# The first w_up weights move into tiles of y that come free earlier, and the first three products begin without the last pair of form tiles

## What is computed

```python
def layer(x, ...):
    h = rmsnorm(x, norm_mix_g)
    proj = einsum('btd,de->bte', h, w_in)
    ...                                   # RG-LRU and pooling branches
    y_mix = concatenate([y_lru, y_pool], axis=-1)
    x = x + einsum('bte,ed->btd', y_mix, w_out)        # w_out: 2048 x 2048
    h2 = rmsnorm(x, norm_mlp_g)
    f = relu(einsum('btd,df->btf', h2, w_up))          # w_up: 2048 x 8192
    x = x + einsum('btf,fd->btd', f * f, w_down)       # w_down: 8192 x 2048
```

## Time and profile before

| | |
|---|---|
| median of three runs | 1935.13 us (1933.71 to 1935.13) |
| the profiled execution | 1937.47 us, span 1935.4 us |
| TensorE matmul busy | 1900.8 us, 98% of the span |
| VectorE busy | 1125.7 us, 58% |
| ScalarE busy | 764.7 us, 40% |
| mean granted TensorE clock | 0.989 |
| w_up begins | 519.07 us into the span |

### The profile page before, as it was taken

How to read it: one execution, slowest core, us unless ns; L and a number is a source line. 1 busy time by engine, 2 the same in 40 slices (tenths; PEclk the granted TensorE clock), 3 DMA queues, 4 the chain that set the end, 5 groups by cost and what they waited for, 6 DMA issues and landing times.

```text
span 1935.4 us, 38521 instructions
## 1 busy us (share of the span) xinstructions
PE 1900.8 (98%) x15746; PEld 1897.7 (98%) x15746; DVE 1125.7 (58%) x1442; ACT 764.7 (40%) x1054; POOL 71.4 (4%) x135
## 2 busy tenths in 40 slices
PE   7999999999899999999999999999999999999997
PEld 7999999999899999999999999999999999999997
DVE  7777775454587777777777775443334444343334
ACT  6555533333344545445454453222222222222234
POOL 2000000200000000000000000000000000000000
PEclk9999999999899999999999999999999999999998
DMA  8233332444444444444444324333444443333333
GB/s 276 88 93 92 93 101 88 151 137 135 149 120 125 142 154 118 143 124 142 132 118 144 122 94 138 115 115 117 125 137 136 135 136 115 116 115 115 93 91 108
DMA packets 202936, 241.36 MB, mean 125 GB/s; under 512 B 10558, under 2 KB 186186, under 8 KB 202769
## 3 DMA queue, kind: packets, MB, share of 16 engines
q1 hardware_dynamic: 187904, 186.87, 32.7%
q0 software_dynamic: 14880, 52.32, 7.2%
HBM read 209.22 MB, written 30.45 MB: 124 GB/s over the span
## 4 chain that ended last, share of the span: by engine, by line
PE 95%; issue 2%; DVE 1%; DMA 1%; ACT 0%; POOL 0%; SPq 0%; ACTq 0%; DVEq 0%; POOLq 0%
PE ps L783 13%; PE ps L781 12%; PE ps L785 12%; PE ps L742 11%; PE ps L744 11%; PE ps L743 11%; PE ps L562 8%; PE ps L565 8%; PE ps L568 8%; PE ps L805 1%; PE ps L579 0%; PE ps L580 0%; PE ps L581 0%; DMA work_area<-in_state_pool_dram 0%; DVE h_low L1384 0%
## 5 line engine op out<-in xcount | busy, mean ns | idle before, releaser
L1712 DVE TENSOR_TENSOR d_low<-d_raw,d_high 128x512 fp32r<-128x512 f32 x256 | 176.7, 691 | 424.8 <-ACT d_high L1079 424.8
L781 PE MATMUL ps<-f_high,d_high 128*128 128x260 f32 x2048 | 411.8, 282 | 4.2 <-DVE resid L1722 4.2
L783 PE MATMUL ps<-f_low,d_high 128*128 128x260 f32 x2048 | 413.5, 283 | 0.0
L785 PE MATMUL ps<-f_high,d_low 128*128 128x260 f32 x2048 | 411.4, 282 | 0.0
L742 PE MATMUL ps<-forms,u_high 128*128 128x260 f32 x1344 | 380.9, 283 | 6.8 <-issue 6.8
L744 PE MATMUL ps<-forms,u_low 128*128 128x260 f32 x1344 | 380.6, 283 | 0.0
L743 PE MATMUL ps<-forms,u_high 128*128 128x260 f32 x1344 | 380.2, 283 | 0.0
L1079 ACT ACTIVATE d_high<-d_raw 128x512 fp32r<-128x512 f32 x256 | 161.5, 632 | 519.0 <-PE ps L785 519.0
L781 PEld LDWEIGHTS ps<-f_high,d_high 128*128 128x128 f32 x2048 | 315.9, 189 | 4.4 <-DVE resid L1722 4.4
L785 PEld LDWEIGHTS ps<-f_high,d_low 128*128 128x128 f32 x2048 | 316.7, 189 | 0.0
L783 PEld LDWEIGHTS ps<-f_low,d_high 128*128 128x128 f32 x2048 | 315.7, 189 | 0.0
(11 more groups left out here) (260 smaller groups left out, 2846.9 us busy)
## 6 DMA issues: line engine op xcount, KB each, us to landing
d_raw<-in_w_down_dram SPq DMA_DIRECT2D x256, 256.0 KB, 2.8
even_rows<-in_w_up_dram SPq DMA_DIRECT2D x32, 1024.0 KB, 6.6
odd_rows<-in_w_up_dram SPq DMA_DIRECT2D x32, 1024.0 KB, 5.7
raw<-in_w_in_dram SPq DMA_DIRECT2D x96, 256.0 KB, 2.8
f_spill<-f_out POOLq DMA_DIRECT2D x32, 520.0 KB, 7.1
scratch<-f_spill POOLq DMA_DIRECT2D x32, 520.0 KB, 4.6
raw<-in_w_out_dram SPq DMA_DIRECT2D x64, 256.0 KB, 2.8
x_spill<-x POOLq DMA_DIRECT2D x8, 520.0 KB, 3.0
```

The source lines that it names most:

```text
L781: pe.matmul(outs[a], wh, fh[:, kk, a * HALF:(a + 1) * HALF], start=opens, stop=False)
L783: pe.matmul(outs[a], wh, fl[:, kk, a * HALF:(a + 1) * HALF], start=False, stop=False)
L785: mm = pe.matmul(outs[a], wl, fh[:, kk, a * HALF:(a + 1) * HALF], start=False, stop=closes)
L1712: dve.tensor_tensor(d_low[:, s].rearrange("p k e -> p (k e)"), d_raw[:, s, :], d_high[:, s].rearrange("p k e -> p (k e)").bitcast(F32), AL ...
```

## The change

`y_high` and `y_low` are laid out anew for what comes after w_out, so that what is written first lies in the slots that come free first: even rows of w_up and weight slot 0 in the first four slots (free after unit 154), forms 6 behind them (free after 156, before 154), odd rows and weight slot 1 behind those (158), forms 7 last (160). The tiles of the later w_down stage move with them. In m=0 product r=3 comes ahead of r=2. Products at places 0, 1 and 2 run over pairs 0 to 6 first, and over pair 7 after all three; only then are their slots released. ScalarE makes weights_high(0) and (1), and VectorE weights_low(0) and (1), before the end of the last unit as far as their waits allow. `block_sums(0,5)` and `block_sums(0,6)` go from turns 3 and 4 to turns 5 and 6.

```diff
+def product_of(q):
+    m, place = divmod(q, PRODUCTS)
+    return m, (0, 1, 3, 2, 4, 5, 6)[place] if m == 0 else place
+def place_of(m, r):
+    return PRODUCTS * m + ((0, 1, 3, 2, 4, 5, 6).index(r) if m == 0 else r)
...
-FREE_Y = 2 * FORM_SET
+ROWS_BYTES = KP * 256 * 4
+FORMS6_AT = ROWS_BYTES
+ODD_AT = FORMS6_AT + -(-FORM_SET // 32) * 32
+FORMS7_AT = ODD_AT + ROWS_BYTES
...
+        even_rows = [at_byte(f"even_rows{b}", at, [P, KP, 256]) for b, at in enumerate((Y_HIGH_AT, W_AT))]
+        odd_rows = [at_byte(f"odd_rows{b}", at, [P, KP, 256])
+                    for b, at in enumerate((Y_HIGH_AT + ODD_AT, W_AT + ROWS_BYTES))]
-        slot_at = (Y_LOW_AT + FREE_Y, Y_LOW_AT + FREE_Y + 2 * KP * P * 4, W_AT + 2 * KP * 256 * 4)
+        slot_at = (Y_LOW_AT, Y_LOW_AT + ODD_AT, W_AT + 2 * ROWS_BYTES)
...   SyncE, rows of w_up
-                        sp.wait_ge(unit_used, 158 if i == 0 else 160)
+                        sp.wait_ge(unit_used, 154 if i == 0 else 158)
...
-                        sp.wait_ge(u_lo, PRODUCTS * (m - 2) + (4 if i == 0 else 7))
+                        sp.wait_ge(u_lo, PRODUCTS * (m - 2) + (7 if i else 6 if m == 2 else 4))
...   TensorE
-                for k in range(KP):
-                    if m == 0 and r == 0:
+                for k in tiles:
+                    if q < SLOTS:
                         pe.wait_ge(s_hi, 2 * k + 2)
                         pe.wait_ge(s_lo, 2 * k + 2)
...
+            for q in range(SLOTS):
+                product(q, range(KP - 1))
+            for q in range(SLOTS):
+                product(q, (KP - 1,))
+            for q in range(SLOTS, PRODUCTS * UP_PAIRS):
+                if q == PRODUCTS:
                     pe.wait_ge(mean_ready, 2)
-                for r in range(PRODUCTS):
-                    product(m, r)
-                    if m == 0 and r == 2:
+                product(q, range(KP))
+                if q == SLOTS:
...                       the L757 matmuls
...   ScalarE
                 if o == 6:
-                    act.wait_ge(unit_used, 154)
+                    act.wait_ge(unit_used, 156)
...
+                    if n == OUT_PAIRS - 1 and j == 6:
+                        weights_high(0)
...
+                    act.wait_ge(unit_used, (154, 158, 160)[q])
...
+            weights_high(1)
             x2_blocks(OUT_PAIRS - 1)
-            weights_high(0)
+            weights_high(2)
             forms_high(OUT_PAIRS - 1)
-            weights_high(1)
             x2_squares(OUT_PAIRS - 1)
-            for turn in range(2, PRODUCTS * UP_PAIRS):
+            copy_p1(0)
+            for turn in range(SLOTS, PRODUCTS * UP_PAIRS):
                 weights_high(turn)
                 up_copies(turn)
...   VectorE
+                    if n == OUT_PAIRS - 1 and j == 7:
+                        block_sums(0, 1)
+                        weights_low(0)
...
+            weights_low(1)
             x2_add(OUT_PAIRS - 1)
+            block_sums(0, 3)
             x2_sums(OUT_PAIRS - 1)
-            block_sums(0, 1)
-            weights_low(0)
+            weights_low(2)
             forms_low(OUT_PAIRS - 1)
-            block_sums(0, 3)
-            weights_low(1)
             squares_add(OUT_PAIRS - 1)
-            for turn in range(2, PRODUCTS * UP_PAIRS):
+            for turn in range(SLOTS, PRODUCTS * UP_PAIRS):
...
-                if r == 3:
+                if place == (3 if m else 5):
                     block_sums(m, 5)
-                if r == 4:
+                if place == (4 if m else 6):
                     block_sums(m, 6)
                 weights_low(turn)
-                if m >= 1 or r == 6:
+                if m >= 1 or place == 6:
                     up_sums(turn)
                 if turn == 5:
                     mlp_norm()
```

More of the change, by code:

```diff
@@ L198, in build @@
         sets = [at_byte(f"forms{o}", o * 2 * FORM_SET, [P, 2, FORMS, HALF], F32R) for o in range(6)]
[L199 to L208, removed]
+        late = [[at_byte(f"forms{o}_{part}", at + place, [P, FORMS, HALF], F32R)
+                 for part, at in (("high", Y_HIGH_AT), ("low", Y_LOW_AT))] for o, place in ((6, FORMS6_AT), (7, FORMS7_AT))]
+        s_high = [v[:, 0] for v in sets] + [v[0][:] for v in late]
+        s_low = [v[:, 1] for v in sets] + [v[1][:] for v in late]
+        even_rows = [at_byte(f"even_rows{b}", at, [P, KP, 256]) for b, at in enumerate((Y_HIGH_AT, W_AT))]
+        odd_rows = [at_byte(f"odd_rows{b}", at, [P, KP, 256])
+                    for b, at in enumerate((Y_HIGH_AT + ODD_AT, W_AT + ROWS_BYTES))]
         t_sum = at_byte("t_sum", AUX_AT, [P, KP, P])
-        slot_at = (Y_LOW_AT + FREE_Y, Y_LOW_AT + FREE_Y + 2 * KP * P * 4, W_AT + 2 * KP * 256 * 4)
+        slot_at = (Y_LOW_AT, Y_LOW_AT + ODD_AT, W_AT + 2 * ROWS_BYTES)
         u_high = [at_byte(f"u_high{b}", at, [P, KP, P], F32R) for b, at in enumerate(slot_at)]
@@ L215, in build @@
         f_out = [at_byte(f"f_out{b}", STAGE_AT + b * PAIR_BYTES, [P, 4, HALF]) for b in range(2)]
-        d_raw = at_byte("d_raw", Y_HIGH_AT + FREE_Y, [P, D_RING, UNIT])
-        d_high = at_byte("d_high", Y_HIGH_AT + FREE_Y + D_RING * UNIT * 4, [P, D_RING, 2, 256], F32R)
-        d_low = at_byte("d_low", Y_HIGH_AT + FREE_Y + 2 * D_RING * UNIT * 4, [P, D_RING, 2, 256], F32R)
+        d_raw = at_byte("d_raw", Y_HIGH_AT, [P, D_RING, UNIT])
+        d_high = at_byte("d_high", Y_HIGH_AT + ODD_AT, [P, D_RING, 2, 256], F32R)
+        d_low = [at_byte(f"d_low{b}", at, [P, 2, 256], F32R)
+                 for b, at in enumerate((Y_HIGH_AT + D_RING * UNIT * 4, Y_HIGH_AT + ODD_AT + D_RING * UNIT * 4,
+                                         Y_HIGH_AT + FORMS7_AT + FORM_SET + 16))]
         window_at = [W_AT] + [b * 2 * PAIR_BYTES for b in range(WINDOW - 1)]
@@ L716, in _, with product @@
                         out_unit(2 * b + half, j, half)
-            def product(m, r):
-                q = PRODUCTS * m + r
+            def product(q, tiles):
+                m, r = product_of(q)
                 form, bank_at = PRODUCT_FORM[r], 4 * (m % 2) + PRODUCT_BANK[r]
@@ L744, in product @@
                     mm = pe.matmul(out, wl, xh, start=False, stop=(k == KP - 1), skip_group_check=True)
-                mm.then_inc(u_used, 1)
-            for m in range(UP_PAIRS):
-                if m == 1:
-                    pe.wait_ge(mean_ready, 2)
-                for r in range(PRODUCTS):
-                    product(m, r)
-                    if m == 0 and r == 2:
[L753 to L759, removed]
+                if tiles[-1] == KP - 1:
+                    mm.then_inc(u_used, 1)
+            for q in range(SLOTS):
[4 more added lines that the diff above has]
+                if q == PRODUCTS:
+                    pe.wait_ge(mean_ready, 2)
+                product(q, range(KP))
+                if q == SLOTS:
+                    pe.wait_ge(sq_summed, OUT_PAIRS)
+                    pe.wait_ge(pair_evac, 12)
+                    for a in range(2):
+                        for t in range(2):
+                            mm = pe.matmul(ps[:, 4 + a, 0:HALF], ones[:], scratch[:, 2 + t, a * HALF:(a + 1) * HALF],
+                                           start=(t == 0), stop=(t == 1))
+                    mm.then_inc(total_ready, 1)
             for u, (seg, kp) in enumerate(D_UNITS):
@@ L777, in _ @@
                     for t in range(2):
-                        wh, wl = (w[:, u % D_RING, kk, t * P:(t + 1) * P] for w in (d_high, d_low))
+                        wh, wl = (w[:, kk, t * P:(t + 1) * P] for w in (d_high[:, u % D_RING], d_low[u % D_RING]))
                         outs = [ps[:, 4 * down_buf(seg) + 2 * t + a, 0:HALF] for a in range(2)]
@@ L994, in forms_high, with weights_high @@
                 act.activation(s_high[o][:, 4:FORMS, :], sums[:], ACT.Copy).then_inc(s_hi, 1)
+            def weights_high(q):
+                m, r = product_of(q)
+                if q < SLOTS:
+                    act.wait_ge(unit_used, (154, 158, 160)[q])
+                else:
+                    act.wait_ge(u_used, q - SLOTS + 1)
+                if r == 0:
+                    act.wait_ge(rows_in[0][m % 2], 16 * (m // 2 + 1))
+                elif r in (2, 4):
+                    act.wait_ge(rows_in[1][m % 2], 16 * (m // 2 + 1))
+                if r in t_ready:
+                    act.wait_ge(t_ready[r], m + 1)
+                act.activation(u_high[q % SLOTS][:], up_block(m, r), ACT.Copy).then_inc(u_hi, 1)
             for n in range(OUT_PAIRS):
@@ L1032, in f_free, with copy_p1 @@
                     act.wait_ge(blocks_ready, 2 * (OUT_PAIRS - 1 + m))
-            def up_copies(q):
-                m, r = divmod(q, PRODUCTS)
-                if r == 3:
[L1038 to L1041, removed]
-                    else:
-                        act.wait_ge(u2_ready, m)
-                    act.activation(p1_copy, ps[:, 4 * (m % 2) + BANK_A, 0:HALF], ACT.Copy).then_inc(p1_copied, 1)
-                if r == 4:
```

(66 more changed lines are left out.)

8 lines of the change are left out of this document (3 added, 5 removed).

## The result

The changed kernel took 1941.22 us (median of 9 runs, 1939.39 to 1943.92) beside 1935.13 us for the kernel before in the same comparison: a ratio of 1.003, 95% interval 1.0022 to 1.0039, 4.3 to 7.5 us. The forecast was 1935.5 us, range 1931.8 to 1938.5. The profiled execution took 1943.92 us, span 1941.9.

The account below looks back on a forecast made before the run. TensorE's matmuls bound the kernel; only waits could be won. Seam before: 6.99 wait + 2.8 clock = 9.8 us; after: 0.81 + 2.16 + 4.41 + clock 2.8 = 10.2. Difference +0.4, forecast 1935.5 us, range 1931.8 to 1938.5.

Parts of the forecast that it names:

- Part 1: End of w_out: weights 0 and 1 made early at no cost, 0.6 us ahead of x2_add(7); products 0, 1 start at once.
- A: TensorE's wait before product 2, for weights_low(2) on VectorE: 0.81 us.
- B: TensorE's wait before product 3, whose weights cannot begin until a slot comes free behind pair 7: 2.16 us.
- C: TensorE's wait before product 6, because block_sums(0,6) stands behind mlp_norm on VectorE: 4.41 us.
- Part 4: TensorE's granted clock at the seam: falls to 1.2 GHz behind C, losing 2.8 us (bounds 0 and 2.8).
- B's clock: Loss by a slow clock behind the wait at product 3: put at 0.
- a wait of 2.1 us: TensorE's existing wait at the kernel's end, after which the clock was read as still 1.00 at 1912 to 1913.
- 0.50 already at 525: Sign of being wrong: granted clock at 0.50 by 525 us, where the forecast had 1.00 from 514 to about 537.
- Rival (c): Seam: B brings the clock down too, C does not shrink; 2.8 us more, 1938.3 us; chance 0.15.
- (a): Seam: the clock does not fall in C, or only for a part; 1932.7 us; chance 0.14.
- The new places of the w_down tiles: w_down: moving its tiles adds or removes no instruction, so 0 us either way.

Follow-up runs that it names:

- e7: The kernel of e2 with a fourth weight slot, used once, for product 3's weights; 1930.77 us, ratio 0.9977 to the kernel before.
- e2: The changed kernel with mlp_norm cut in three, its later operations moved behind turns 12 and 19; 1934.44 us, ratio 0.9994 to the kernel before.
- e1: The kernel before with only the tile layout of the changed kernel, every order of work as before; 1939.01 us beside 1935.51, ratio 1.0019.
- e5: The kernel of e2 with all that the change put into y_high and y_low 96 bytes further on; 1933.56 us, ratio 0.9988 to the kernel before.
- e6: The kernel of e2 with w_down's tiles dealt out otherwise in the same regions; 1934.78 us, ratio 0.9992 to the kernel before.
- e8: The kernel of e7 with the 96 bytes of e5 and the w_down arrangement of e6; 1931.77 us, ratio 0.9981 to the kernel before.
- e3: The changed kernel with w_down's tiles back where they lay before, its first three loads waiting for w_up's end; 1947.81 us, ratio 1.0056 to the kernel before.
- e9: As e8 with 32 bytes in place of 96; 1930.75 us in one execution, its places then timed at 1928.87 us, ratio 0.9968 to the kernel before.

## Why the prediction was wrong

- **Part 1, weights 0 and 1 early: right.** forms_high(6) waited until 501.28, both conversions kept their cover, weights_low(1) ended 1.0 us ahead of x2_add(7).
- **Stalls A, B, C: right to 0.2 us each.** Forecast 0.81, 2.16 and 4.41; measured 0.8, 2.2 and 4.5. The causes are the ones named: e7 removes B with a slot, e2 removes C by moving the norm.
- **Part 4, the clock: half right.** C lost 2.35 us (2.8 forecast; the clock was back just before the end of product 6). B's clock was put at 0, by the likeness to a wait of 2.1 us. In three of the five profiled kernels with a stall B it fell, at 1.4 us in after, so that one of the prediction's own signs of being wrong, 0.50 already at 525, came true. The reading behind the 0 stopped too soon. The earlier trace rows ends at 1913; 1 us further on the same trace has:

```profile
1914.00:1916.00 2.00, 2.00 (x14) 2.00 (x12) 0.32 (x2) 1.98 (x3) 0.00 (x0) 0.57 0.00 0
```

The clock is at 1.2 GHz from 1914.3 until about 1924.5, and in all 13 traces it has fallen at most 3.2 us after the end of that wait. (The matmuls there are short ones, 128x1 and 128x128, so it is open whether the wait or they brought it.) Rival (c) was given 0.15; it was nearer one half. The clock behind the old wait is not fixed either, 2.8 us before and 1.6 in e1. The Trainium skill (TensorE: Matmul & The Clock Gate, "What's actually happening") says that the monitor runs free of the kernel; that the same stall did and did not bring the clock down agrees with this, but the two chips leave room for another reason. The prediction put the spread from (a) to (c) at some 3 us; by its own times it is 5.6, and the nine runs of after spread over 4.5.

- **The failed step: "The new places of the w_down tiles add or remove no instruction ... 0 either way"**, and the silence on w_up's. It measured 3.3 us in w_down and 0.8 in w_up (spacing), 3.5 us together by e1's median. With it and half of B's clock the sum is 0.4 + 0.7 + 4.1 = 5.2 us, 1940.3, inside the measured interval (4.3 to 7.5 us slower); the 0.9 left to the medians' 6.1 no run assigns. Without it even rival (c), 1938.3, was too low. I had taken a matmul's spacing as a constant of the engine, from 71 matmuls of one layout. The Trainium skill (SBUF — State Buffer, "SBUF: two separate sides") says that TensorE's own ports wait for nobody, and (TensorE: Matmul & The Clock Gate, "Step-by-step: what each phase is for") that a weight load takes nothing from a running matmul's reads; neither lets one expect that a place has a price, and the measurements decide.

What stays open is the mechanism. It isn't the remainder modulo 128 bytes (e5), nor only the scattering of d_low (e6), and offset and arrangement act together: in w_down 96 bytes cost 0.03 ns in the arrangement of after (e5) and 0.56 in that of e6 (e8). Nor is it one kind of matmul: from before to after the second of two on a low weight goes from 118.8 to 120.3 ns behind the first and `f_high` by `d_high` pairs from 119.3 to 119.0, while in e8 the pair of `f_low` by `d_high` has 122.3. Whether it is the two reads of TensorE that meet, or its reads and other engines' writes, no run here tells apart.

## What to carry to other kernels

When tiles move, compare the count of matmuls in equal stretches at the same granted clock, in stages that the change doesn't otherwise touch: a fraction of a nanosecond a matmul over 11,000 of them is as much as a stall, and no wait shows it. When a wait is opened by starting work without its last inputs, look at once for what that work now holds (here all three slots) and for what lies behind it in an engine's list (here a 6 us norm that three products used to cover); both could be read off the trace of before to 0.2 us. A stall of 2 us may or may not cost the clock on top (three profiles of five here), so price it at half and put both ends into the range; and when a wait is read as one that left the clock alone, read the rows of the next few us too.

## What the runs showed of the hardware

- The mean spacing of 128x260 matmuls at 2.4 GHz depends on where operands lie in SBUF: 119.47 to 120.42 ns in w_down over eight layouts, 119.82 to 120.07 in w_up. For one layout it repeats from kernel to kernel to 0.01 ns or so (120.01 in after, e1, e2, e7; 119.48 and 119.47 in before and e3; 119.65 twice for the places of e9).
- Moving operands by 32 bytes, with nothing else changed, took w_down from 119.48 to 119.65 ns.
- The same 2.0 us stall behind the same work was followed by a granted clock of 0.50 in three profiles (after, e2, e3) and by 1.00 in two (e5, e6, on another chip than e2 and e3).
- The same wait of 6.83 us at product 0 was followed by 2.8 us of loss by the slow clock in before and 1.6 in e1.
